# A one-core hybrid decoder step: the second sample stage with paired query products, window attention ahead of memory attention, one output scale from a bound and an output in three parts

## The reference

```python
z = rms_norm(x, norm_b[j]) @ w_in_b[j]
q, gq, qm, gm = jnp.split(z, [SWA_W, 2 * SWA_W, 2 * SWA_W + MEM_W], axis=-1)
q = rope_partial(rms_norm(q.reshape(B, T, N_Q_HEADS, HEAD_DIM), q_norm[j]), pos)
o = swa_window(q, k_all, v_all, pos, k_pos, sinks[j])      # 12 heads, 4 key/value heads, 128 old + 8 new keys
ys = o * jax.nn.silu(gq)
ym = memory_branch(qm, gm, mem_q_norm[li], mem_k[li], mem_v[li])
x = x + jnp.concatenate([ys, ym], axis=-1) @ w_out_b[j]
```

## Time and profile before

| what | value |
| --- | --- |
| median of 3 executions | 1689.85 us (1685.21 to 1691.19) |
| the profiled execution, own time | 1692.14 us |
| its span, first to last instruction | 1690.4 us |
| mean granted TensorE clock | 0.967 |
| PE busy | 1546.4 us (91%) |
| DVE, ACT, POOL busy | 834.1, 544.2, 505.7 us |
| DMA moved | 127.38 MB, mean 75 GB/s |

### The profile page before, as it was taken

One profiled execution on the slowest core, in us unless ns is written; L12 is line 12 of the kernel. 1 busy time (PEld: TensorE's weight loads), 2 busy tenths in 40 slices (PEclk: granted clock), 3 DMA queues, 4 the chain that ended last, 5 costly groups with the idle time before them and its releaser, 6 DMA issues.

```text
span 1690.4 us, 32455 instructions
## 1 busy us (share of the span) xinstructions
PE 1546.4 (91%) x12867; PEld 1184.8 (70%) x12867; DVE 834.1 (49%) x1777; ACT 544.2 (32%) x1352; POOL 505.7 (30%) x369
## 2 busy tenths in 40 slices
PE   5848999999999999978999999999999999999976
PEld 3627888887888888864766757667476675767744
DVE  3856554555455455433634636346263462735522
ACT  2353241322324233221524315143151431614330
POOL 0116333444434335231323223232232322214110
PEclk9879999999999999998999999999999999999986
DMA  9043121221312213295010010100101001010040
GB/s 389 32 150 119 56 102 63 88 100 66 135 51 100 76 76 129 80 382 235 2 51 1 1 51 1 51 1 1 51 1 51 1 1 51 1 51 1 5 181 26
DMA packets 25121, 127.38 MB, mean 75 GB/s; under 512 B 2455, under 2 KB 3095, under 8 KB 12518
## 3 DMA queue, kind: packets, MB, share of 16 engines
q1 hardware_dynamic: 24830, 124.88, 19.1%
q10 hardware_dynamic: 144, 0.37, 0.1%
HBM read 87.64 MB, written 39.74 MB: 75 GB/s over the span
## 4 chain that ended last, share of the span: by engine, by line
PE 40%; issue 23%; DVE 16%; POOL 13%; ACT 6%; DMA 1%; POOLq 0%; DVEq 0%; SPq 0%; ACTq 0%
PE ps_z L655 16%; PE ps_z L689 14%; PE ps_z L666 3%; ACT ph_sb L1462 3%; DVE ph_sb L2082 2%; POOL w_x_sb L2295 2%; DVE tiny_sb L2085 2%; DVE ph_sb L2109 2%; POOL ph_sb L2360 2%; POOL tiny_sb L2264 1%; POOL ph_sb L2358 1%; POOL big_sb L2269 1%; DVE xn_sb L1608 1%; DVE tiny_sb L1672 1%; PE ps_p L1034 1%
## 5 line engine op out<-in xcount | busy, mean ns | idle before, releaser
L666 PE MATMUL ps_z<-xn_sb,w_in_sb 128*128 128x256 f16 (+1 forms) x4752 | 502.4, 264 | 12.9 <-DVE gate_sb L1687 6.7
L666 PEld LDWEIGHTS ps_z<-xn_sb,w_in_sb 128*128 128x128 f16 x4752 | 426.0, 98 | 76.6 <-issue 15.1
L689 PE MATMUL ps_z<-pm_sb,w_out_sb 128*128 128x256 f16 x3072 | 349.5, 274 | 16.5 <-DVE gate_sb L1687 16.5
L689 PEld LDWEIGHTS ps_z<-pm_sb,w_out_sb 128*128 128x128 f16 x3072 | 299.6, 99 | 57.4 <-DVE gate_sb L1687 18.7
L2264 POOL TENSOR_TENSOR tiny_sb<-tiny_sb 128x8 f32<-128x8 f32 (+5 forms) x74 | 108.6, 1468 | 609.6 <-DVE tiny_sb L1654 302.8
L655 PE MATMUL ps_z<-w_in_sb,xn_sb 128*128 128x512 f16 (+2 forms) x840 | 181.7, 376 | 0.0
L1198 ACT ACTIVATE scr_sb<-ps_z,tiny_sb 128x256 f32<-128x256 f32 (+2 forms) x94 | 42.6, 490 | 377.6 <-PE ps_z L655 296.8
L655 PEld LDWEIGHTS ps_z<-w_in_sb,xn_sb 128*128 128x128 f16 (+1 forms) x840 | 82.9, 99 | 94.1 <-issue 0.2
L1645 DVE TENSOR_REDUCE tiny_sb<-scr_sb 128x8 f32<-128x512 f32 (+3 forms) x64 | 38.0, 593 | 221.1 <-ACT scr_sb L1198 139.3
L1728 DVE SCALAR_TENSOR_TENSOR x_buf_sb<-ps_z,tiny_sb,x_buf_sb 128x512 f32<-128x512 f32 x64 | 48.0, 750 | 120.0 <-PE ps_z L689 120.0
L655 PE MATMUL ps_z<-w_x_sb,xn_sb 128*128 128x512 f16 (+1 forms) x408 | 93.7, 391 | 10.8 <-issue 5.8
(11 more groups left out here) (287 smaller groups left out, 2109.5 us busy)
## 6 DMA issues: line engine op xcount, KB each, us to landing
x_buf_sb<-x SPq DMA_DIRECT2D x18, 1024.0 KB, 5.0
w_x_sb<-w_b SPq DMA_DIRECT2D x18, 1024.0 KB, 6.3
x<-x_buf_sb SPq DMA_DIRECT2D x9, 1024.0 KB, 4.1
y<-x_buf_sb SPq DMA_DIRECT2D x9, 1024.0 KB, 3.9
parts<-ph_sb SPq DMA_DIRECT2D x16, 512.0 KB, 3.0
parts<-w_x_sb SPq DMA_DIRECT2D x16, 512.0 KB, 3.6
w_in_sb<-parts SPq DMA_DIRECT2D x8, 1024.0 KB, 10.9
w_out_sb<-w_mem SPq DMA_DIRECT2D x4, 1024.0 KB, 18.6
```

Source lines behind the costliest of these rows:

```text
L666: last = mm(ps_z[:, b, half * NT:half * NT + n], w_split[:, g, ws, kc, half * P:(half + 1) * P], xs[:, x, kc, 0:n], start=(kc == 0 and ws ...
L689: done = mm(ps_z[:, b, half * NT:(half + 1) * NT], w_out_split[:, g, ws, kc, half * P:(half + 1) * P], gated_parts[:, x, kc, :], start=sta ...
```

## The change: what it does

In `SB`:

- The query products come first. The tokens' 64 rows are used twice: groups 0 and 1 of the query weights go to rows 0 to 63 of a bank and groups 2 and 3 to rows 64 to 127 (`qab`), product by product in turn. The heads are then finished as 8 heads on 128 rows: rows 64 to 127 take the units of heads 8 to 15, and the four memory queries among them are written again, without rotation. Four transposes of 128 x 128 take the place of eight of 64 x 128, and ten copies that of twelve.
- Window scores come ahead of memory scores, all eight sequences at once, and the softmax of the window weights goes by halves of four sequences. VectorE multiplies them by the inverse sums, GpSimd only copies the columns of the new keys.
- The memory weights are no longer multiplied by their inverse sum; the copy of the memory values takes it as its scale. This is so in `SA` too.
- One scale serves the whole output. It comes from a bound: the largest gate, times a bound on the values from the sums of squares of the two memory-value quads, the largest new value and the largest old value. The gates are multiplied by their unit ahead of it.
- The old values' products come before those of the new keys in each half. The output is accumulated in one bank in three parts: chunks 6 and 7, 0 to 2, 3 to 5.
- The old keys are loaded after the last window values of the prompt, the first memory-key quad after `qab`, the second after the store of `y`.

```diff
-            "SB": ["kv0", "qa0", "qb0", "gm", *G3, "out0", "out1"],
+            "SB": ["qab", "kv0", "gm", *G3, "out"],
...
-            "SB": ["kT", "qT00", "qT01", "pt0", "pt1", "vt", "ptw0", "ptw1", "ptn", "top0", "top1"],
+            "SB": ["qT0", "kT", "pt0", "pt1", "ptw0", "ptw1", "top0", "ptn", "vt"],
...
+            V.wait_full(sp, "B", TILES - 1, "pvw5")
+            dma(kT_all[:, :, :, 0:BLK], io["kc"]).then_inc(kold_in, 16)
+            Z.wait_full(sp, "SB", 0, "qab")
+            load_quad("SB", 0)
             sp.wait_ge(x_stored.sem, x_stored.after("B", TILES - 1))
-            load_quad("SB", 0)
-            dma(kT_all[:, :, :, 0:BLK], io["kc"]).then_inc(kold_in, 16)
-            Z.wait_full(sp, "SB", 0, "qa0")
             load_quad("SB", 1)
+            Z.wait_full(sp, "SB", 0, "kv0")
             dma(v_old, io["vc"]).then_inc(vold_in, 16)
...
+            for kc in range(KC):
+                for ws, x in PARTS:
+                    for half in range(2):
+                        last = mm(ps_z[half * NS:(half + 1) * NS, b, :].rearrange("p (g n) -> p g n", g=2),
+                                  xs[:, x, kc, 0:NS], w_split[:, 2 * half:2 * half + 2, ws, kc, :],
...
             split_tokens("SB", 0, "kv0", 0, w_kv, (0, 1), NS)
-            split_tokens("SB", 0, "qa0", 0, w_split, (0, 1), NS)
-            split_tokens("SB", 0, "qb0", 0, w_split, (2, 3), NS)
             split_features("SB", 0, "gm", 7, NS)
+            split_features("SB", 0, "g0", 4, NS)
...
+            old_transposes(0)
+            sample_mem_values("SB")
+            old_transposes(1)
+            pe.wait_ge(top_sum.sem, top_sum.after("SB", 0))
+            T.wait_free(pe, "SB", 0, "top0")
+            mm(ps_t[:, 0:4], ones[:, :], tops[:, 0:4], start=True, stop=True).then_inc(T.full[0], 1)
...
+            old_values(0)
+            sample_value_transposes("SB")
+            old_values(1)
+            for i in range(3):
+                back_outputs(i)
...
+            old_exps(0)
             sample_mem("SB")
-            act.wait_ge(w_neg_in.sem, w_neg_in.after("SB", 0))
-            for n in range(DB):
...
+            from_t("SB", 0, "pt0", pt_s[:, 0, :], ps_t[:, 0:NMEM])
+            old_exps(1)
+            from_t("SB", 0, "pt1", pt_s[:, 1, :], ps_t[:, 0:NMEM])
...
+            for i in range(2):
+                act.wait_ge(quad_in[2 + i].sem, quad_in[2 + i].after("SB", 0))
+                last = f((big, xn)[i][:, :, :], QUADS["SB"][2 + i].rearrange("p (k n) -> p k n", k=KC), ACT.Square,
+                         accum_out=tops[:, 2 + i:3 + i])
...
+            row_top_of("SB", 0, 0, row_tops[:, 0, :], gate[:, :, 0:NS])
+            own(ve.tensor_reduce(row_tops[0:NS, 1, 1:2], v[0:NS, 0, :], AX.X, ALU.max, apply_absolute_value=True))
+            dve.wait_ge(vold_in, 16)
+            own.wait()
+            row_top_of("SB", 0, 1, row_tops[:, 1, 0:1], v_old.rearrange("p b n -> p (b n)"))
...
+            back_low(0)
+            old_gated(0)
+            back_low(1)
+            old_gated(1)
+            back_low(2)
...
-            sample_mem_norm("SA")
```

More of the change, by code:

```diff
@@ L918, in sample_mem_transposes @@
             def sample_mem_transposes(part):
[L919 removed]
+                S.wait_read(pe, part, 0, "m")
                 for mc in range(MC):
@@ L1121, in _, with back_outputs @@
                     project_out("B", t, (2, 3))
-            pe.wait_ge(xlow_in.sem, xlow_in.after("SB", 0, -1))
+            def back_outputs(i):
+                pe.wait_ge(gated_low.sem, gated_low.after("SB", 0, i))
+                b = Z.wait_free(pe, "SB", 0, "out") if i == 0 else Z.bank("SB", "out")
+                for c in range(KC):
+                    for kc in BACK[i]:
+                        for ws, x in PARTS:
+                            end = i == 2 and c == KC - 1 and kc == BACK[i][-1] and ws == 1
+                            last = mm(ps_z[:, b, c * NS:(c + 1) * NS],
+                                      w_out_split[:, c // 2, ws, kc, (c % 2) * P:(c % 2 + 1) * P], gated_s[:, x, kc, :],
+                                      start=(i == 0 and c == 0 and kc == BACK[i][0] and ws + x == 0), stop=end,
+                                      skip_group_check=True)
+                if i == 2:
+                    last.then_inc(Z.full[b], 1)
@@ L1130, in _ @@
+            last.then_inc(T.full[0], 1)
+            split_features("SB", 0, "g1", 5, NS)
+            split_features("SB", 0, "g2", 6, NS)
+            pe.wait_ge(heads_norm.sem, heads_norm.after("SB", 0, 1))
             T.wait_free(pe, "SB", 0, "kT")
@@ L1134, in _ @@
             last.then_inc(T.full[0], 1)
[L1135 to L1141, removed]
+            T.wait_read(pe, "SB", 0, "kT")
             b = S.wait_free(pe, "SB", 0, "w")
@@ L1155, in _, with old_transposes @@
             last.then_inc(V.full[0], 1)
+            sample_mem_scores("SB", qbd_b)
             sample_mem_transposes("SB")
[L1157 to L1160, removed]
+            def old_transposes(half):
+                pe.wait_ge(pw_norm.sem, pw_norm.after("SB", 0, half))
                 T.wait_free(pe, "SB", 0, f"ptw{half}")
@@ L1271, in sample_values @@
                 V.wait_full(act, part, 0, "pvm")
-                f(values_s, ps_p[:, :].rearrange("p (c n) -> p c n", c=2), ACT.Copy).then_inc(V.free[0], 1)
+                act.wait_ge(m_inv_in.sem, m_inv_in.after(part, 0))
+                for half in range(2):
+                    last = f(values_s[:, half, :], ps_p[:, half * NMEM:(half + 1) * NMEM], ACT.Copy,
+                             scale=m_inv[:, 0, half:half + 1])
+                last.then_inc(V.free[0], 1)
             def sample_row_squares(part, i):
@@ L2181, in _, with norms, pair @@
             own.end_loop(TILES)
-            k_heads("SB", 0, 0, None, NS)
+            for blk in range(NBLK):
+                dve.wait_ge(heads_norm.sem, heads_norm.after("B", TILES - 1, 1 + blk))
+            ve.tensor_copy(unit_heads[HD:P, 0:8], unit_heads[HD:P, 8:16]).then_inc(pair_units, 1)
+            dve.wait_ge(scr_in.sem, scr_in.after("SB", 0, 0))
+            b = Z.bank("SB", "qab")
+            q = q_of(0)
+            own(ve.tensor_reduce(q_ss[:, 0:8], scr[:, b, :].rearrange("p (h d) -> p h d", h=8), AX.X, ALU.add))
+            def norms(r, heads, lower):
+                a = SMALL["row"][0] + r * HD
+                n = P - HD if lower else P
+                return small[P - n:P, a:a + HD].rearrange("p (h d) -> p h d", h=1).to_broadcast([n, heads, HD])
+            def pair(lo, at, h):
+                return ps_z[lo:P, b, at:at + h * HD].rearrange("p (h d) -> p h d", h=h)
+            ve.tensor_tensor(q[:, 0:4, :], pair(0, 0, 4), norms(ROW_Q, 4, False), ALU.mult)
+            own(ve.tensor_tensor(q[:, 4:8, :], pair(0, 256, 4), norms(ROW_Q, 4, False), ALU.mult))
+            own(variance(q_ss[:, 0:8], q_rstds[0][:, 0:8]))
+            rotate(q[:, 0:8], 8, sm("cos_s"), sm("sin_s")).then_inc(heads_var.sem, 1)
+            dve.wait_ge(heads_var.sem, heads_var.after("SB", 0, 0))
+            ve.tensor_tensor(q[HD:P, 4:8, :], pair(HD, 256, 4), norms(ROW_MEMQ + 1, 4, True), ALU.mult)\
+                .then_inc(Z.free[b], 1)
+            Z.wait_read(dve, "SB", 0, "qab")
+            ve.memset(w_flat[:, 0:2048], 0.0).then_inc(qbd_zero.sem, 1)
+            dve.wait_ge(scr_in.sem, scr_in.after("SB", 0, 1))
+            head_group("SB", 0, "kv0", 1, k_ss[0:NS, 0:4], [(k_tok[0:NS, 0], 0, 4, ROW_K)], NS)
             Z.wait_read(dve, "SB", 0, "kv0")
```

252 lines of the change are left out of this document (152 added, 100 removed).

## The result

The changed kernel takes **1670.79 us** (median of 6 runs, 1664.89 to 1677.41) where the kernel before takes 1690.76 beside it (6 runs, 1685.21 to 1700.75). The ratio is 0.9856 with a 95% interval of 0.9826 to 0.9887, so between 19 and 29 us are gone. The forecast was 1668.7, in a range of 1663 to 1678.

A forecast was written before the change was run, and what follows sets the result against it. The second sample stage was taken as one chain of waits across engines, worth at most 87 us; 14.2 (front) + 7.0 (back) = 21.2 us off 1689.85 gave 1668.7, range 1663 to 1678.

The forecast's parts named there:

- front: Second sample stage until its last window score ends (1603.9 to 1641.6): 23.5 us against 37.7, 14.2 saved.
- back: Second sample stage from the last window score's end to the last output product: 36.3 us against 43.3, 7.0 saved.
- Query products: Second sample stage's 48 query products, alternating row halves: 0.119 us each, 5.7 us, against 10.5 before.
- Rival 1: Weight loads are exposed beside the paired query products, so pairing gains nothing: 10.5 us, 1673.5 in all; 10%.
- GpSimd off the chain: GpSimd's query-head work takes 3.0 us against 5.2, ready at 1616.4, so it leaves the second sample stage's chain.
- Scores at the full clock: Second sample stage's 16 window products at 0.28 us each: 4.5 us, ending at 1627.4; 7.5 at 1.2 GHz.
- The bound is hidden: VectorE's 4.9 us before the softmax hide behind window scores; ScalarE's squares, done 1640.5, behind memory values ending 1640.6.
- Rival 3: The value-cache load or the squares of the memory-value quads decide: +1 to 5 us, 1670 to 1674; 12%.
- Outputs: The 192 output products ending the second sample stage: 6.2 us, between 5.2 all fast and 10.4 all slow.
- The first sample stage is worth nothing: Dropping GpSimd's 1.03 us product there gains nothing: TensorE reached its transposes after it ended; scaled copies cost at most 0.2.
- Rival 2: Clock worse than taken: scores at 1.2 GHz +3.0, outputs all slow +4.2, gates +1 to 3; 1676 to 1679; 15%.
- Rivals 4 and 5: 4: row-half changes stall TensorE, 1706 us, 2%; 5: an unseen wait eats most of the saving, 1682 to 1690, 6%.

The follow-up runs named there:

- fillers: 28 products of no use put into TensorE's pauses late in the second sample stage of the changed kernel: 1665.69 us, ratio 0.9819 to the kernel before.

## Why the prediction was right, and where it was off

The forecast for the stage was a saving of 21.2 us, the profiles show 22.8 (81.1 to 58.3), and the timed ratio says 19 to 29. The kind and the mechanism of the front hold, and the range held the time. In the back the sum came out (36.2 us against 36.3) although one of its terms did not: there the agreement is luck of the clock. Step by step:

- **Query products**, 48 x 0.119 = 5.7: measured 5.37, 0.112 each. The row of the prompt tiles' memory values was the right one. Rival 1 falls: the records of the weight loads (48 of 0.110 us each, two at a time, so 2.6 us of busy time) lie wholly beside the products. The rows of the kernel before could have ruled it out already: 24 unpaired products took 5.4 us there, 0.218 each, with 24 loads of 0.110 us of the same row group beside them; with the loads exposed it would have been 8.0. So the rule in "TensorE: Matmul & The Clock Gate", part 3 (The mechanism), of the Trainium skill, loads overlap only where the row group differs, does not hold here; the trace disagrees with it. The same section also lets a load for the array's background weight buffer run ahead of the products, which would fit; no run here tells whether it is that.
- **GpSimd off the chain**: it had the query heads ready 12.5 us into the stage as forecast (1.64 us of power, then 0.20 and 1.04), and no instruction of the front waits for it. The wait for the key/value bank, forecast 0.3, is 0.56.
- **Scores at the full clock**, 4.5: measured 3.96 (3.02 + 0.94 in the chain). The clock was 1.00 through the whole front. The front took 22.0 us instead of 23.5; the difference is 0.4 in the query products, 0.5 in the scores, and the rest in small steps between, the 2.96 us of gates 1 and 2 among them.
- **The bound is hidden**, by nothing to spare: its reading is, by 0.1 and 0.2 us, and taking that away brings nothing. Its sum and short steps, about 1 us, are on the path, as the forecast had them. Rival 3 falls here and becomes true as soon as the clock is full in the back, as the sentence on the squares said: the fillers hand the chain to them.
- **Back**: from the first exp to the end of the memory values 9.8 (forecast 10.4), from there to the old values 2.5 (2.9), the first half with the transposes 5.4 (6.3), gating 2.5 (2.5), second half 5.2 (5.2). What is shorter lies mostly in and around the stretch at 1.00 near 1645, which I had not forecast; in the profile with little of the bound, which lacks such a stretch, the memory values take 3.7 instead of 3.4 us and the first half 5.2 instead of 4.6, without its transposes.
- **Outputs**, 6.2: measured 7.75. This is the term that was mis-sized, by 1.6 us. I had let the clock return some 7 us into a stretch of unbroken work, from the one case in the trace of before, and had counted the old values into that stretch. Here TensorE worked without a gap from 1654.49 and the clock came back 9.7 us later. With half 0 gated first (the single execution) it had worked without a gap from 1650.66, and the clock was back only some 16 us later:

```profile
1664.00:1666.00 2.00, 2.00 (x42) 2.00 (x40) 0.15 (x1) 0.00 (x0) 0.00 (x0) 0.50 0.02 4
1666.00:1668.00 2.00, 2.00 (x62) 2.00 (x60) 0.00 (x0) 0.00 (x0) 0.00 (x0) 0.82 0.05 8
```

  So the 7 us were no measure. In the nine profiles of the changed kernel and its variants without fillers the return lay 3.8 to 6.0 us behind the first output product, and the outputs took 7.5 to 8.5 us. The error of 1.6 us was cancelled within the back by the shorter steps above; the 1.6 us by which the stage is shorter than forecast come from the front (22.0 against 23.5).
- **The first sample stage is worth nothing**: wrong in its reason. I asked only whether TensorE waited for GpSimd's product, and not what it did to VectorE beside it. The edit takes 0.75 us off a wait on the chain; what the clock does behind it is larger than that. The Trainium skill says in "SBUF — State Buffer", Who interferes with whom, that a VectorE instruction with two inputs in SBUF contends with a GpSimd instruction that reads SBUF, one of them blocked until the other is done. The row of 1048 ns agrees with that, and I had not drawn on it.
- **The sum against the time**: the two profiled executions differ by only 17.4 us (1692.14 and 1674.72), since the stage starts 5.4 us later. In the profiles of this study it starts between 1600.2 and 1612.8, with the same work before it, so this is spread. The time of a single execution can't be read closer than that; the stage's own length can.

Rival 2, a clock worse than forecast, took place at the outputs only, and there with 1.6 of its 4.2 us. Rivals 4 and 5 did not.

Not tried: clearing the block-diagonal queries on another engine, which would take away the wait of 0.56 us for the key/value bank; and squares made cheaper beside full-clock memory values.

## What to carry to other kernels

Products like these, with 64 output rows, can be issued in pairs on the two row halves of one bank at nearly half the price each (0.112 us against 0.218), if they alternate; in this stage that paid only with the finishing of their result beside other products. Price a moved or removed step by what it does to every engine beside it, VectorE under GpSimd above all, and not only by who waits for its result. In a tail with pauses put first what frees the next stretch of TensorE's work, then ask whether filling the pauses pays: here the two brought 7 us of the stage together, and the step that was just hidden before became the next bound.

## What was not expected of the hardware

- One VectorE step with two inputs in SBUF took 1048 ns instead of 272 beside a GpSimd product of 1.03 us.
- At a single change of the row half the neighbours overlap too: four pairs at each of two changes, 0.9 us each, so 1.7 us of the expected 5.2 stayed saved.
- The clock can fall in the middle of busy work, some time after a pause. In the profile with fillers TensorE had waited 1.17 and 0.60 us before 1644.35 and worked without a gap from there, and the windows show:

```profile
1644.00:1646.00 2.00, 1.78 (x16) 1.79 (x17) 1.50 (x5) 0.00 (x0) 0.70 (x1) 1.00 0.00 0
1646.00:1648.00 2.00, 2.00 (x6) 0.87 (x6) 0.68 (x4) 0.00 (x0) 0.00 (x0) 0.55 0.03 8
```

  Nine fillers that followed took 4.05 us at 1.2 GHz and held up real work by about 1.1 us; the clock was back some 7 us after its fall. With three fillers there, and half 0 gated first, the stage was 1.3 us shorter still; the two edits were not separated.
- Two profiles with the same TensorE instructions and waits (the changed kernel and the one with little of the bound) agreed to 0.01 us through 30 us, and then differed by 1.8 us, with the clock low for 6.8 us less in the first. Two profiles of the changed kernel itself gave 58.3 us both.
